# Another order of the tensors in the on-chip memory, and a 64-byte filler left out

## What is computed

```
h = rms_norm(x, mix_norm[l]);  a, b, p, gc, gp = split(h @ w_in[l])          # 512, 512, 512, 1024, 1024 columns
u = causal depthwise convolution (31 taps) of a * sigmoid(b), + bias
yc = silu(layer_norm(u)) @ w_conv_out[l]
yp = (moving averages of p over 2, 4, 8, 16 positions, minus p) @ w_pool[l] * pool_scale[l]
x += (sigmoid(gc) * yc + sigmoid(gp) * yp) @ w_out[l]
h = rms_norm(x, ffn_norm[l])
layer 0: x += (silu(h @ w_gate) * (h @ w_up)) @ w_down                        # dense, 2816 wide
layer 1: x += sum over the token's top 2 of 8 experts of p_e * swiglu_e(h)    # each 3584 wide
out = rms_norm(x, final_norm)
```

## Time and profile before

| | us |
|---|---|
| median of 3 runs (lowest, highest) | 1507.37 (1507.27, 1507.77) |
| the profiled execution | 1507.77 |
| its span, first to last instruction | 1506.0 |

### The profile page before, as it was taken

One profiled execution on the slowest core, in us unless ns is written; L12 is line 12 of the kernel. 1 busy time (PEld: TensorE's weight loads), 2 busy tenths in 40 slices (PEclk: granted clock), 3 DMA queues, 4 the chain that ended last, 5 costly groups with the idle time before them and its releaser, 6 DMA issues.

```text
span 1506.0 us, 18439 instructions
## 1 busy us (share of the span) xinstructions
PE 1458.6 (97%) x6617; PEld 1200.0 (80%) x6617; DVE 1193.4 (79%) x979; ACT 993.0 (66%) x880; POOL 152.0 (10%) x236
## 2 busy tenths in 40 slices
PE   7989999999989899999999999999999999999997
PEld 5877888888867688888888888878888888888885
DVE  4767554455867798998899899899889889889986
ACT  5665534435764577767777777776777777777764
POOL 6860400000760000000000000000000000000000
PEclk9999999999999799999999999999999999999999
DMA  9445555555336489999899899998988989999890
GB/s 351 158 139 181 184 182 195 189 175 193 123 117 238 173 324 394 345 341 379 339 357 365 335 364 356 356 385 328 385 346 338 383 333 365 357 356 382 332 369 29
DMA packets 186224, 434.42 MB, mean 288 GB/s; under 512 B 7825, under 2 KB 11201, under 8 KB 186177
## 3 DMA queue, kind: packets, MB, share of 16 engines
q1 hardware_dynamic: 184704, 432.20, 77.1%
q10 hardware_dynamic: 1472, 1.61, 0.3%
HBM read 432.73 MB, written 1.05 MB: 288 GB/s over the span
## 4 chain that ended last, share of the span: by engine, by line
PE 81%; POOL 6%; DVE 4%; issue 4%; ACT 3%; DMA 0%; POOLq 0%; SPq 0%; DVEq 0%; ACTq 0%
PE bank L1108 25%; PE bank L1110 25%; PE bank L1109 25%; POOL work L450 4%; PE bank L1257 2%; ACT w_hi L511 2%; DVE w_lo L765 2%; POOL gates L406 1%; DVE dT_lo L1032 1%; PE bank L1328 1%; PE bank L1353 1%; POOL mix L423 1%; PE bank L1354 0%; DVE xs L892 0%; PE bank L1336 0%
## 5 line engine op out<-in xcount | busy, mean ns | idle before, releaser
L765 DVE TENSOR_TENSOR w_lo<-raw,w_hi 128x2048 fp32r<-128x2048 f32 x315 | 716.9, 2286 | 241.6 <-ACT w_hi L511 240.7
L511 ACT ACTIVATE w_hi<-raw 128x2048 fp32r<-128x2048 f32 x315 | 602.5, 1918 | 361.2 <-PE bank L1110 354.3
L1108 PE MATMUL bank<-w_hi,dT_hi 128*128 128x512 f32 (+1 forms) x912 | 360.7, 395 | 8.2 <-DVE w_lo L765 3.7
L1110 PE MATMUL bank<-w_hi,dT_lo 128*128 128x512 f32 (+1 forms) x912 | 355.0, 389 | 0.0
L1109 PE MATMUL bank<-w_lo,dT_hi 128*128 128x512 f32 (+1 forms) x912 | 354.6, 389 | 0.0
L1108 PE MATMUL bank<-w_hi,cT_hi 128*128 128x512 f32 x568 | 223.4, 393 | 0.0
L1110 PE MATMUL bank<-w_hi,cT_lo 128*128 128x512 f32 x568 | 221.3, 390 | 0.0
L1109 PE MATMUL bank<-w_lo,cT_hi 128*128 128x512 f32 x568 | 221.1, 389 | 0.0
L1108 PEld LDWEIGHTS bank<-w_hi,dT_hi 128*128 128x128 f32 x912 | 172.0, 189 | 47.9 <-issue 6.6
L1110 PEld LDWEIGHTS bank<-w_hi,dT_lo 128*128 128x128 f32 x912 | 171.8, 188 | 36.2
L1109 PEld LDWEIGHTS bank<-w_lo,dT_hi 128*128 128x128 f32 x912 | 172.0, 189 | 33.5
(11 more groups left out here) (189 smaller groups left out, 1282.9 us busy)
## 6 DMA issues: line engine op xcount, KB each, us to landing
raw<-in_moe_w_gate_dram SPq DMA_DIRECT2D x96, 1024.0 KB, 7.0
raw<-in_moe_w_up_dram SPq DMA_DIRECT2D x72, 1024.0 KB, 8.7
raw<-in_moe_w_down_dram SPq DMA_DIRECT2D x72, 1024.0 KB, 7.3
raw<-in_w_in_dram SPq DMA_DIRECT2D x28, 1024.0 KB, 5.3
mix<-in_moe_w_up_dram SPq DMA_DIRECT2D x16, 1024.0 KB, 8.8
gates<-in_moe_w_down_dram SPq DMA_DIRECT2D x16, 1024.0 KB, 9.4
gates<-in_moe_w_up_dram SPq DMA_DIRECT2D x16, 1024.0 KB, 9.0
work<-in_moe_w_down_dram SPq DMA_DIRECT2D x16, 1024.0 KB, 9.3
```

Of the source, the lines that this page charges most:

```text
L511: act.activation(w_hi[:, u % SPLIT, 0:width], place[slot][:, 0:width], ACT.Copy).then_inc(hi_ready, 1)
L765: dve.tensor_tensor(w_lo[:, u % SPLIT, 0:width], place[slot][:, 0:width], w_hi[:, u % SPLIT, 0:width].bitcast(F32), ALU.subtract).then_inc ...
L1108: nc.tensor.matmul(dst, a_hi, b_hi, start=start, stop=False)
L1110: return nc.tensor.matmul(dst, a_lo, b_hi, start=False, stop=stop)
```

## The change

The declarations change their order. The filler `to_512` is gone; `vecs` and `small` move from the front to behind `mean_w`; `items` moves to the very end; `mix` moves from behind `mean_w` to between `tokP` and `tap_prod`. No instruction is added, removed or moved, and no shape changes: the addresses of the operands are all that differs.

```
-        vecs = sb("vecs", [P, 56])
-        small = sb("small", [P, 16])
-        items = sb("items", [P, 8], I32)
-        sb("to_512", [P, 16])
         raw = sb("raw", [P, RAW, UNIT])
         w_hi = sb("w_hi", [P, SPLIT, UNIT], F32R)
...
         tokP = sb("tokP", [P, TB, N])
+        mix = sb("mix", [P, CC * (PAD + S) + GROUPS * (2 * P + REACH)])
+        u_end, b_end = CC * (PAD + S), CC * (PAD + S) + GROUPS * (P + REACH)
+        uT = mix[:, 0:u_end].rearrange("p (c t) -> p c t", c=CC)
+        band_0 = mix[:, u_end:b_end].rearrange("p (g t) -> p g t", g=GROUPS)
+        band_1 = mix[:, b_end:].rearrange("p (g t) -> p g t", g=GROUPS)
         tap_prod = sb("tap_prod", [P, PRODS, S])
...
         mean_w = sb("mean_w", [P, P])
-        mix = sb("mix", [P, CC * (PAD + S) + GROUPS * (2 * P + REACH)])
...
+        vecs = sb("vecs", [P, 56])
         taps = sb("taps", [P, 2, 124])
+        small = sb("small", [P, 16])
         rw = sb("rw", [P, KD, E])
...
         comb_of = sb("comb_of", [P, TABLE * TB])
+        items = sb("items", [P, 8], I32)
```

## The result

The changed kernel takes 1530.49 us (median of 4 runs, 1527.32 to 1533.24) against 1507.32 us before (4 runs, 1507.26 to 1507.77): 23 us longer, a ratio of 1.0154 with a 95% interval of 1.0138 to 1.0172. The forecast was 1507.9 us in a range of 1503 to 1530.

What follows compares the result with a forecast made beforehand. PE was taken to set the pace, with the transfers hidden behind it. PE, DVE, ACT and POOL added 0, transfers 0.5 us at the start: 1508.3 us profiled, 1507.9 as median, range 1503 to 1530.

Steps and rivals of the forecast that it cites:

- What bounds the kernel: Whole kernel: PE sets the pace, busy 1458.6 of 1506.0 us; with the experts no transfer stands among the releasers of waits.
- The transfers: Writes to starts off the grid: between 0 and 1.3 us at the kernel's start, hidden behind PE with the experts.
- The middle estimate: Transfers: one more packet's fixed part, 8 ns, for each run; 116.9 us an item, below the period of 123.5.
- the reserve of 14%: Experts: an item's transfers take 108.2 us of its 123.5 us period, leaving 15.3 us.
- the 0.5 us of the sum: Kernel start: the transfers' cost taken from between 0 and 1.3 us, the only nonzero term.
- The first rival: Experts: each run off the grid costs 512 bytes more and transfers become the bound; about +31 us, 1538; chance 0.17.
- VectorE, ScalarE, GpSimd: Experts and mixers: moved operand starts cost 0; bounds 0.4 us for DVE's taps, 0.3 us for POOL's adds.
- TensorE: PE's matmuls and weight loads: moved starts cost 0; bound 1 ns on 6617 matmuls, 6.6 us either way.
- The second: Engines' own reads slower off the grid: 1 to 3 ns a matmul, 6.6 to 20 us, 1514 to 1527; chance 0.12.
- The third: PE's two reads: leaving the grid shared with w_hi, w_lo frees 1 ns a matmul, 6.6 us, 1501; chance 0.09.
- the faster case: Whole kernel faster by over 3 us, chance 0.09; 0.04 of it left outside the range's lower end, 1503.

Runs made afterwards that it cites:

- e12: The kernel before with 256 bytes behind w_lo: w_hi and w_lo at 0, every stationary operand at 256 past a multiple of 512; 1507.74 us, 1.0003.
- e7: The kernel before with the 64 bytes of to_512 moved behind raw: raw alone starts 448 past a multiple of 512; 1507.98 us, 1.0002.
- e5: The kernel before with to_512 deleted: every tensor from raw to mix starts 448 past a multiple of 512; 1507.9 us, 0.9998.
- e6: The kernel before with to_512 made 32 bytes longer: every tensor from raw to mix starts 32 past a multiple of 512; 1507.69 us, 0.9999.
- e2: The kernel before with to_512's 64 bytes moved behind tokP: raw, w_hi, w_lo, hT and others at 448, cT and dT at 0; 1531.18 us, 1.0163.
- e9: The kernel before without to_512, 128 bytes behind tokP: w_hi, w_lo, hT at 448, cT and dT at 64; 1528.16 us, 1.0128.
- e8: The kernel before with cT_hi, cT_lo, dT_hi, dT_lo at 0, 64, 128 and 192, w_hi and w_lo at 0; 1526.55 us, 1.0128.
- e11: The kernel before with only w_lo moved, to 64; w_hi at 0, stationary operands at 256; 1532.23 us, 1.0153.
- e10: The kernel before with w_hi and w_lo in one tensor, both at 16, everything behind them at 32; 1545.36 us, 1.0244.
- e1: The changed kernel with a 32-byte filler behind mix, so that cT, dT and the rest start at 384; 1507.5 us, 1.0003 to the kernel before.

## Why the prediction was wrong

**What bounds the kernel: right.** PE set the pace before and does after; nothing took that place.

**The transfers: right in cost and in cover.** The middle estimate was 8 ns more for a packet, the measured one about 5 in 17:32 (with the reservation of e12); the reserve of 14% with the experts held it, as foreseen. At the start of the kernel ACT's timeline after the change shows what it did, against the earlier trace rows:

```profile
10.35 1.91 ACT L526 ACTIVATE w_hi<-raw 128x2048 fp32r<-128x2048 f32 x1 [5.83 <-DMA raw<-in_w_in_dram]
...
16.04 1.91 ACT L526 ACTIVATE w_hi<-raw 128x2048 fp32r<-128x2048 f32 x1
18.24 1.92 ACT L526 ACTIVATE w_hi<-raw 128x2048 fp32r<-128x2048 f32 x1 [0.28 <-DMA raw<-in_w_in_dram]
...
22.41 1.92 ACT L526 ACTIVATE w_hi<-raw 128x2048 fp32r<-128x2048 f32 x1
```

The second and third copies end at 20.16 in place of 19.15, one us late, but the fourth starts at 22.41, earlier than the 23.69 of before, so that the 0.5 us of the sum weren't paid. The Trainium skill's rule ("DMA: Bandwidth & Descriptors", "How a descriptor splits into AXI transactions"), carried over to writes, had given an estimate of 12.5% for 2 KB; the measured packets of e7 in 17:32 are 6% longer, and the measurement decides. The first rival, the transfers as the bound, did not happen: e7 moves `raw` alone and shows no loss (1.0002).

**VectorE, ScalarE, GpSimd: right.** Their rows are the same to 1 or 2 ns at the median: POOL's adds 737 against 738, DVE's splits 2292 both times.

**TensorE: the step that failed.** The sum had 0 here, "a moving operand off the grid costs 0, with 3 ns as the widest spread", and for the stationary one "a load would have to grow by 37 ns, a fifth, before PE's pace changed". Both sentences look at one operand at a time. In their own terms they are even true: e5 and e6 move every operand off the grid and lose nothing, and the weight load kept its 187 or 188 ns in the slow kernels. What the runs show in their place is a relation between the operands: matmuls of this fp32r form start 5 to 6 ns further apart unless the stationary and the moving operand start at the same byte modulo 256. Distances of 0 and 256 were free; 16, 32, 64, 128 and 224 cost time, and so did the kernels that mix in 96, 160 and 192. Other distances weren't tried. The change took `cT` and `dT` 224 bytes away from `w_hi` and `w_lo`. 4440 matmuls have them as stationary operand ((912 + 568) x 3 by the page). Added up behind these, the distances under 300 ns from one start to the next come to 982.2 us before and 1005.8 us after: 23.6 of the 24.0 us.

That PE's own two reads are what meets is argued by this: while a matmul runs, the weights of the next are loaded, and in the changed kernel the places where `hT` and `cT` take turns show which matmul pays.

```profile
202.73 0.40 PE L1125 MATMUL bank<-w_hi,hT_lo 128*128 128x512 f32 x1
202.73 0.19 PEld L1123 LDWEIGHTS bank<-w_hi,cT_hi 128*128 128x128 f32 x1
...
213.93 0.39 PE L1125 MATMUL bank<-w_hi,cT_lo 128*128 128x512 f32 x1
213.93 0.19 PEld L1123 LDWEIGHTS bank<-w_hi,hT_hi 128*128 128x128 f32 x1
```

The first works with `hT_lo`, which agrees with `w_hi`, and takes 396 ns while `cT_hi` is loaded; the second works with the mismatched `cT_lo` and takes 389 ns while `hT_hi` is loaded. So it is in all seven places where `cT` or `dT` follows `hT` and in all four where `hT` follows `cT`; in the kernel before, all eleven take 389 ns. In e2, however, at a distance of 64, the same places read the other way round: 388 ns with `hT_lo`, 392 with `cT_lo`. And in e9, at 128, both kinds take 395 or 396 ns. Both the load under way and the weights in use can matter, then, and what decides between them isn't known.

Line 1208 misled because it is another form, float32 of 256 columns. The starts of its two operands differ by 240 + 4j bytes modulo 256 for tap j, so that one of its 16 taps (j = 4) has agreeing starts, and that one isn't faster than the others. The starts of these matmuls do lie 215 to 219 ns apart, nearly the same at the same tap in every group of 16, so the form isn't indifferent to the start; but agreement isn't what it follows. Why wasn't tried. The distance of 225 ns in the prediction was two gaps of the earlier trace rows read to a hundredth of a us; over six gaps it is 227 (e5, below).

**The rivals.** The second, slower reads of the engines, had the right place and the right sign ("an unchanged stream with matmul starts further apart than 225 ns") and was given 0.12; its size was taken from the spread of line 1208, 1 to 3 ns, and was 6. The upper end of the range, 1530, came from 3 ns on all 6617 matmuls; that the measured 1530.49 lies next to it is luck, since it is 5 to 6 ns on 4440. (The range's lower end is said to give away "the larger part" of the faster case, but 0.04 of 0.09 is the smaller.) The third named the mechanism that fits best, PE's two reads disturbing each other, and had its sign backwards: it took the shared grid of before for the disturbed state, and it is the undisturbed one. Any of the experiments' fast kernels has that sharing, and none is faster than before, so no run shows anything to gain.

**What stays open.** How a mismatch of one operand reaches its neighbours (e8, e11), and whether the load under way or the weights in use count; what slows the first transfers of e12; why 16 bytes cost more than 32 (e10). And the changed kernel's runs spread over 1527 to 1533 us; those of before did so over 0.5 us in the same comparison, but over 1504 to 1510 in those of the experiments. In 425:434 the profiled run of the changed kernel has a granted clock of 0.64, a dip to the lower level of 1.2 GHz for part of the stretch (in 418:427, mostly ahead of it, PE was busy for 5.53 of 9 us); the same place before has 1.00:

```profile
425.00:434.00 9.00, 6.24 (x15) 4.51 (x16) 3.25 (x7) 1.54 (x3) 6.73 (x8) 0.64 0.35 117
```
```profile
421.00:430.00 9.00, 3.78 (x16) 2.65 (x15) 4.72 (x7) 2.85 (x6) 8.14 (x9) 1.00 0.37 127
```

The 6617 matmuls of both kernels come in the same order, so their starts can be compared one by one. Where the kernel before is at 40 us, the changed one is 1.4 us ahead; at 413 us it is 1.3 us behind, at 441 us 3.2. So the stretch of the dip holds 1.9 of the 3.5 us that were lost ahead of the experts, and the 408 matmuls with `cT` or `dT` there hold 2.1 (their distances add up to 89.1 us in place of 87.0); less the 1.4 won at the start, some 0.9 us stay unattributed. But the dip isn't a cost of the addresses that were compared: e1, which has no slow matmul and takes 1507.5 us, has it too, and loses 1.8 us over the same matmuls.

```profile
421.00:430.00 9.00, 6.75 (x16) 4.93 (x17) 3.05 (x6) 1.66 (x2) 6.51 (x8) 0.62 0.34 117
```

## What to carry to other kernels

When a layout changes, don't ask operand by operand whether it is aligned; ask which two streams one engine reads at the same time, and whether their starts still agree. Here the stationary and the moving operand of back-to-back fp32r matmuls (128 x 128 weights, 512 columns) had to start at the same byte modulo 256, and a 32-byte filler in the right place was worth 1.5% of a kernel that PE bounds. And a row that is flat over all starts speaks for its own form of instruction only.

## What was not expected of the hardware

A weight load of 128 x 128 and the matmul that runs beside it aren't independent: 227 ns (1.36 us for six starts in e5, below) from one start to the next with agreeing starts, 233 ns in the changed kernel, while the load itself stays at 187 or 188 ns at the median.

```profile
902.76 0.39 PE L1107 MATMUL bank<-w_hi,cT_hi 128*128 128x512 f32 x1
...
904.12 0.39 PE L1107 MATMUL bank<-w_hi,cT_hi 128*128 128x512 f32 x1
```

The Trainium skill says in "SBUF — State Buffer", section "Who interferes with whom", that TensorE's two read ports are independent and that PE never waits on anyone. For time that doesn't hold here: the runs show that 6 ns of a matmul depend on how the two operands lie to each other, and the measurement decides. Transfers of 2 KB runs to starts off the multiples of 512 (32, 128 and 448 were tried) moved 386 or 387 GB/s in 17:32 in place of 409, 5 ns more a packet; e12 moved 387 there too with `raw` on a multiple, so that the slower packets with the experts (34% of them in e7, 0.1% before) are the better evidence.
